# A two-block hybrid network on one core: TensorE's filler products around five of its norms are left out

## The chip, the core and the metric

The kernel runs on one core of a Trainium2 chip, in one launch. The metric is the time of one execution on the device, in microseconds (us). Single executions of this kernel before the change took 2808.08 to 2811.28 us. The engines are TensorE (PE in the profile, PEld for its weight loads), VectorE (DVE), ScalarE (ACT), GpSimd (POOL) and SyncE (SP), which issues the weight transfers.

## What is computed

Two blocks over one sequence of 512 tokens and 1024 channels, in float32:

```
first_block:   h = rmsnorm(x, norm_mix);  proj = h @ w_in
               mixed = gate0 * (mamba2(...) @ w_ssm_out) + gate1 * (dilated_attention(...) @ w_att_out)
               x = x + mixed @ w_mix_out
               h = rmsnorm(x, norm_ffn)
               x = x + (silu(h @ w_ffn_gate) * (h @ w_ffn_up)) @ w_ffn_down
               x = rmsnorm(x, norm_final)                              # norm 2
second_block:  a = diff_attention(rms_norm(h, a_norm_pre)) @ w_o
               h = h + rms_norm(a, a_norm_post)                        # norm 4
               f = conv_ffn(rms_norm(h, ffn_norm_pre[0]))
               h = h + rms_norm(f, ffn_norm_post[0])                   # norm 6
               a = forgetting_attention(rms_norm(h, b_norm_pre), k, v, c) @ w_o
               h = h + rms_norm(a, b_norm_post)                        # norm 8
               f = conv_ffn(rms_norm(h, ffn_norm_pre[1]))
               out = h + rms_norm(f, ffn_norm_post[1])                 # norm 10
rmsnorm(x, g) = x * rsqrt(mean(x * x over channels) + eps) * g
```

The kernel counts its eleven norms from 0 to 10. The even ones from 2 on are norms of a projection's output (or, norm 2, of the stream after one); each of them but the last is followed at once by an odd norm, whose output is the operand of the next projection.

## The kernel before

Activations stay in SBUF with channels on the partitions: XT is 8 chunks of 128 channels by 512 tokens. A projection runs in panels of 256 output columns; its weights come in slabs of two chunks (SyncE, into `raw`), and GpSimd splits each slab into a rounded high part `whi` (L556) and the rest `wlo` (L558), in four slots. TensorE makes each product of float32 operands as three (high by high, low by high, high by low), so a chunk of a panel is six products of 128x512 (L598, in `chunk`). A slot comes free when TensorE is through with the slab (`slab_done`), and only then does GpSimd split the next.

The order on each engine is written out by hand; semaphores join the engines. Around an even norm k it is as follows. After each panel of the projection VectorE takes the result out of PSUM (L1721 for norm 2, L1760, to `branch`, for the others), ScalarE squares it (L991) and VectorE adds the squares in `acc` (L1341). TensorE then sums acc over the partitions in `sum_squares` (L655, AUX bank 3), ScalarE takes the root (`std`, L999), VectorE the reciprocal (`rstd_col`, L1348), and TensorE spreads the factors over the partitions in `spread` (L667, AUX bank 3 again). Then comes a chain over the eight chunks. In norm 2 VectorE scales the chunk in place (XT, L1752); in the others it scales the branch (L1765) and adds it to the stream (XT, L1767). ScalarE makes the high part of the next operand (`opA_hi`, L995) and the squares for the odd norm; VectorE makes the low part (`opA_lo`, L1332) and adds the squares. That is three VectorE operations a chunk in norm 2 and four or five in norms 4, 6 and 8; in norm 10 two, and the chunk is stored.

TensorE takes the chunks as they come, in `twin_mm`, which runs two panels side by side so that each chunk of the operand feeds both (for norm 6 the second panel is the narrow one of the forget gates). After the first panel's last chunk it makes the odd norm's sum_squares, then the second panel's last two chunks, then the odd norm's spread.

`keep_warm(n)` issues n products of an identity with the attention mask (both bfloat16, 128x512) into an AUX bank that nothing reads then. They wait for nothing and nothing waits for them, but TensorE's queue is in order, so what stands behind waits until they are through. `branch_norm` puts 14 before sum_squares, 15 between sum_squares and spread and 14 after spread. Other calls put 9 behind the odd norms' spread and 7 in places of the attention stages; six products of another kind start the kernel.

Of the kernel before, what the change touches and what calls it, by code (L numbers as in the profile page):

```python
# [23 lines left out]
WARM_SQUARES, WARM_FACTORS, WARM_RESIDUAL, WARM_BANKS, WARM_UNIT = 14, 15, 14, 9, 7  # L24
# [224 lines left out]
def build(nc, I, out):  # L249
    ctx = ExitStack()  # L250
    with ctx:
# [318 lines left out]
        def _(pe):  # L570
# [78 lines left out]
            def sum_squares(k):  # L649

                if k == 0:
                    pe.wait_ge(first_in, 16 * N_FIRST)
                pe.wait_ge(acc_ready, DC * (k + 1))
                for t in range(NB):
                    last = nc.tensor.matmul(AUX[:, 3, t:t + 1], acc[:, t * P:(t + 1) * P], ones[:, 0:1], start=True, stop=True)  # L655
                last.then_inc(ss_done, 1)

            def keep_warm(n, bank=0):

                for _ in range(n):  # L660
                    nc.tensor.matmul(AUX[:, bank, :], ident_bf[:], mask1[:, 0:S], start=True, stop=True)  # L661

            def spread(k):

                pe.wait_ge(rstd_ready, k + 1)
                for t in range(NB):
                    last = nc.tensor.matmul(AUX[:, 3, t * P:(t + 1) * P], rstd_col[:, t:t + 1].broadcast_to([P, P]), ident[:], start=True, stop=True)  # L667
                last.then_inc(bc_done, 1)

            def branch_norm(k):  # L670

                keep_warm(WARM_SQUARES)
                sum_squares(k)
                keep_warm(WARM_FACTORS)
                spread(k)
                keep_warm(WARM_RESIDUAL)

            def after_norm(key, k, panels):

# [164 lines left out]
            for n in range(4):  # L844
                panel_mm("down1", n)
            branch_norm(2)


# [78 lines left out]
            for n in range(2, 4):  # L927
                panel_mm("awo", n)
            branch_norm(4)
            after_norm(("fin", 0), 5, 2 * FP)  # L930
            for n in range(4):
                panel_mm(("fout", 0), n)
            branch_norm(6)

            twin_mm(("k3", 0), 7)
# [1037 lines left out]
```

## Time and profile before

| | us |
|---|---|
| median of three runs (2808.08, 2810.1, 2811.28) | 2810.1 |
| the profiled execution's own time | 2811.09 |
| its span in the trace | 2809.3 |
| TensorE busy | 2638.3 (94%) |
| GpSimd busy | 1616.1 (58%) |
| VectorE busy | 1479.3 (53%) |
| ScalarE busy | 705.3 (25%) |
| mean granted TensorE clock, share of full | 0.964 |

The page gives each engine's busy time as a share of the span, and below that the chain of work that ended last: from the last instruction back, at each step to what released it. A share of the chain by line says how much of the span hangs on that line. Busy shares are means over stages with different limits, so what a change in one stage is worth is read in that stage, in the order of time. Times in rows are from the start of the span. The ends of TensorE's products are modelled: rows of neighbouring products overlap, and their distance from start to start is their rate. A product of float32 operands that is not split takes two or more passes, so the four products of sum_squares and of spread are eight records each. Some records of products are missing.

### The profile page before, as it was taken

Reading aid. Unit: us, or ns where it says so; the run is one execution under the profiler, and the core shown is the slowest. Engines: PE = TensorE matmul, PEld = TensorE weight load, DVE = VectorE, ACT = ScalarE, POOL = GpSimd, SP = SyncE. Lnnn points to the kernel's source line nnn. Section 1 sums busy time; section 2 is a strip of 40 time slices with the busy share of each in tenths; the row PEclk is TensorE's granted clock in tenths of the full one; section 3 lists DMA queues with packets and bytes.
Section 4 is the critical chain, followed back from the end, with each engine's and each line's share of the span. In section 5 each row is a group of like instructions: output and inputs, shape, how many; then the busy total and the mean of one; then the engine's idle time right before and its main releaser. Section 6 shows DMA issues by size and latency. Waiting matters only on the chain.

```text
span 2809.3 us, 37473 instructions
## 1 busy us (share of the span) xinstructions
PE 2638.3 (94%) x12925; PEld 2135.0 (76%) x12948; DVE 1479.3 (53%) x2085; ACT 705.3 (25%) x1251; POOL 1616.1 (58%) x1548
## 2 busy tenths in 40 slices
PE   8878889998999999999999799999989999999998
PEld 6667777787877878888777568888766776688886
DVE  5677677453423523320467668882164445687722
ACT  2233333101123111110234424331022222233300
POOL 5534454574444767777544257887653332588874
PEclk9989899999999999999999899999999999999999
DMA  4433232232222333333312123333221211233331
GB/s 136 121 79 85 70 94 80 75 95 63 68 59 65 117 89 97 96 99 95 101 61 64 35 65 89 96 97 98 76 72 61 61 61 35 63 97 97 96 97 58
DMA packets 235781, 229.17 MB, mean 82 GB/s; under 512 B 15808, under 2 KB 228288, under 8 KB 235664
## 3 DMA queue, kind: packets, MB, share of 16 engines
q1 hardware_dynamic: 212224, 204.72, 25.3%
q10 hardware_dynamic: 23440, 22.82, 2.9%
q8 instruction: 82, 1.34, 0.2%
q14 instruction: 35, 0.29, 0.0%
HBM read 222.67 MB, written 4.82 MB: 81 GB/s over the span
## 4 chain that ended last, share of the span: by engine, by line
PE 72%; DVE 7%; issue 2%; ACT 1%; DVEq 0%; ACTq 0%
PE PS L598 57%; PE PS L592 5%; PE AUX L861 2%; PE AUX L910 1%; PE AUX L813 1%; DVE acc L1341 1%; PE AUX L661 1%; PE AUX L900 1%; DVE opA_lo L1332 1%; DVE branch L1765 1%; PE AUX L915 1%; PE AUX L832 1%; PE AUX L822 0%; PE AUX L864 0%; PE AUX L655 0%
## 5 line engine op out<-in xcount | busy, mean ns | idle before, releaser
L556 POOL TENSOR_SCALAR whi<-raw 128x512 fp32r<-128x512 f32 x772 | 557.0, 722 | 1097.2 <-issue 546.6
L558 POOL TENSOR_TENSOR wlo<-raw,whi 128x512 fp32r<-128x512 f32 x772 | 1059.9, 1373 | 64.5
L598 PE MATMUL PS<-opA_hi,whi 128*128 128x512 f32 x1904 | 764.1, 401 | 34.5 <-DVE opA_lo L1332 22.0
L598 PE MATMUL PS<-opA_hi,wlo 128*128 128x512 f32 x1904 | 749.1, 393 | 0.0
L598 PE MATMUL PS<-opA_lo,whi 128*128 128x512 f32 x1904 | 748.5, 393 | 0.0
L598 PEld LDWEIGHTS PS<-opA_hi,whi 128*128 128x128 f32 x1904 | 362.6, 190 | 128.8 <-DVE opA_lo L1332 22.3
L598 PEld LDWEIGHTS PS<-opA_hi,wlo 128*128 128x128 f32 x1904 | 361.5, 190 | 77.8
L598 PEld LDWEIGHTS PS<-opA_lo,whi 128*128 128x128 f32 x1904 | 362.5, 190 | 72.6 <-issue 0.9
L1789 DVE SCALAR_TENSOR_TENSOR facc<-fu,vec,facc 128x512 f32<-128x512 f32 x176 | 202.1, 1204 | 52.7 <-ACT facc L1221 52.7
L592 PE MATMUL PS<-whi,opA_hi 128*128 128x256 f32 x704 | 211.1, 300 | 1.4 <-DVE y_ssm L1559 1.0
L598 PE MATMUL PS<-hid_hi,whi 128*128 128x512 f32 x528 | 205.4, 389 | 0.0
L598 PE MATMUL PS<-hid_lo,whi 128*128 128x512 f32 x528 | 205.4, 389 | 0.0
L598 PE MATMUL PS<-hid_hi,wlo 128*128 128x512 f32 x528 | 205.4, 389 | 0.0
L592 PE MATMUL PS<-whi,opA_lo 128*128 128x256 f32 x704 | 203.3, 289 | 0.0
L592 PE MATMUL PS<-wlo,opA_hi 128*128 128x256 f32 x704 | 203.0, 288 | 0.0
L592 PEld LDWEIGHTS PS<-whi,opA_hi 128*128 128x128 f32 x704 | 140.1, 199 | 10.3 <-issue 5.6
L592 PEld LDWEIGHTS PS<-whi,opA_lo 128*128 128x128 f32 x704 | 139.8, 199 | 2.4 <-issue 2.3
L1760 DVE COPY branch<-PS 128x512 f32<-128x512 f32 x32 | 20.6, 686 | 227.8 <-PE PS L598 227.8
L592 PEld LDWEIGHTS PS<-wlo,opA_hi 128*128 128x128 f32 x704 | 139.3, 198 | 0.0
L1249 ACT ACTIVATE sc<-sc,bstat 128x128 f32<-128x128 f32 (+3 forms) x128 | 70.8, 554 | 208.1 <-DVE bstat L1850 208.1
L598 PEld LDWEIGHTS PS<-hid_hi,wlo 128*128 128x128 f32 x528 | 99.1, 188 | 20.7
L598 PEld LDWEIGHTS PS<-hid_lo,whi 128*128 128x128 f32 x528 | 99.1, 188 | 20.5
(282 smaller groups left out, 3482.3 us busy)
## 6 DMA issues: line engine op xcount, KB each, us to landing
raw<-in_w_in_dram SPq DMA_DIRECT2D x184, 256.0 KB, 2.7
raw<-in_ffn_w_in_dram SPq DMA_DIRECT2D x176, 256.0 KB, 2.7
raw<-in_ffn_w_out_dram SPq DMA_DIRECT2D x88, 256.0 KB, 2.8
raw<-in_a_w_qkv_dram SPq DMA_DIRECT2D x48, 256.0 KB, 2.7
raw<-in_w_ffn_gate_dram SPq DMA_DIRECT2D x44, 256.0 KB, 2.8
raw<-in_w_ffn_up_dram SPq DMA_DIRECT2D x44, 256.0 KB, 2.7
raw<-in_w_ffn_down_dram SPq DMA_DIRECT2D x44, 256.0 KB, 2.7
acs_row<-acs_dram ACTq DMA_DIRECT2D x16, 512.0 KB, 5.7
```

The costliest lines, as they stand in the source:

```text
L556: nc.gpsimd.tensor_scalar(whi[slot][:], raw[raw_slot][:], 1.0, 1.0, ALU.mult, ALU.mult).then_inc(w_high, 1)
L558: nc.gpsimd.tensor_tensor(wlo[slot][:], raw[raw_slot][:], whi[slot][:].bitcast(F32), ALU.subtract).then_inc(slab_split, 1)
L592: last = nc.tensor.matmul(psum_tm(key, panel)[:, t, :], a, b[:, c, :], start=t % 2 == 0 and k + n == 0, stop=k == total - 1 and n == 2, sk ...
L598: last = nc.tensor.matmul(psum_fm(key, panel, m), a, b[:, k, :], start=k + n == 0, stop=k == total - 1 and n == 2)
L661: nc.tensor.matmul(AUX[:, bank, :], ident_bf[:], mask1[:, 0:S], start=True, stop=True)
L813: nc.tensor.matmul(AUX[:, bank, 0:width], q1[j][:, 2 * gi + hh, q0:q0 + P], k1[j][:, 2 * gi + hh, k0:k0 + width], start=True, stop=False)
L832: last = nc.tensor.matmul(AUX[:, 2, 0:P], probT[:, n, :], v1[j][:, b, gi * PANEL + hh * P:gi * PANEL + (hh + 1) * P], start=n == 0, stop=n ...
L861: last = nc.tensor.matmul(AUX[:, e, 0:width], q2[j % 2][rows, hh, q0:q0 + P], k2[j % 2][rows, hh, 0:width], start=True, stop=True)
L900: last = nc.tensor.transpose(AUX[:, 2 + e, b * P:(b + 1) * P], src, ident[:])
L910: last = nc.tensor.matmul(AUX[:, 2, e * 64:e * 64 + 64], pT[:, e, b, :], v2[j % 2][:, b, hh * P + e * 64:hh * P + e * 64 + 64], start=b == ...
L1249: A(sc[:, u % 2, e, 0:width], sc[:, u % 2, e, 0:width], ACT.Exp, bias=bstat[:, u % 4, 2 + e:3 + e], accum_out=bstat[:, u % 4, 4 + e:5 + e] ...
L1789: V.scalar_tensor_tensor(facc[:, j, :], fu[:, j, tap:tap + S], col("ffn_conv_w_2", 132 * l + 44 * tap + FT * half + m + 2 * i), facc[:, j, ...
```

## The change

The three calls of keep_warm in `branch_norm` are left out. branch_norm is called for norms 2, 4, 6, 8 and 10. The fillers of the odd norms and of the attention stages stay.

```diff
             def branch_norm(k):
 
-                keep_warm(WARM_SQUARES)
                 sum_squares(k)
-                keep_warm(WARM_FACTORS)
                 spread(k)
-                keep_warm(WARM_RESIDUAL)
```

TensorE's order at norm 2, behind down1, before the change (whi and wlo are slots of split weights, hid the hidden activations, opA the next operand):

```order
L598 MATMUL PS<-hid_hi_146,wlo3_64 128x512
L661 MATMUL AUX<-mask1_83,ident_bf_84 128x512 x14
L655 MATMUL AUX<-ones_69,acc_72 128x1 x4
L661 MATMUL AUX<-mask1_83,ident_bf_84 128x512 x15
L667 MATMUL AUX<-ident_68,rstd_col_75 128x128 x4
L661 MATMUL AUX<-mask1_83,ident_bf_84 128x512 x14
L598 MATMUL PS<-opA_hi_65,whi0_57 128x512
```

The same place in TensorE's order after it:

```order
L598 MATMUL PS<-hid_hi_146,wlo3_64 128x512
L655 MATMUL AUX<-ones_69,acc_72 128x1 x4
L667 MATMUL AUX<-ident_68,rstd_col_75 128x128 x4
L598 MATMUL PS<-opA_hi_65,whi0_57 128x512
```

Norms 4, 6 and 8 read alike, norm 10 without the last row. No other engine's order has moved, and the sums, the spread and the products of the projections stand in the order in which they stood.

## Rows read from the trace of the kernel before

**Rows 1.** The page: busy time and instructions by engine; the chain by line.
```profile
PE 2638.3 (94%) x12925; PEld 2135.0 (76%) x12948; DVE 1479.3 (53%) x2085; ACT 705.3 (25%) x1251; POOL 1616.1 (58%) x1548
...
PE PS L598 57%; PE PS L592 5%; PE AUX L861 2%; PE AUX L910 1%; PE AUX L813 1%; DVE acc L1341 1%; PE AUX L661 1%; PE AUX L900 1%; DVE opA_lo L1332 1%; DVE branch L1765 1%; PE AUX L915 1%; PE AUX L832 1%; PE AUX L822 0%; PE AUX L864 0%; PE AUX L655 0%
```
**Rows 2.** The chain in order of time at norm 2: start, us, what.
```profile
1344.91 4.77 PE PS L598 x21
...
1354.30 3.26 PE AUX L661 x15
```
**Rows 3.** TensorE's timeline at norms 2 and 3: start us, us, engine, line, operation.
```profile
1349.74 2.97 PE L661 MATMUL AUX<-mask,ident_bf 128*128 128x512 bf16 x13
1353.24 1.05 PE L655 MATMUL AUX<-ones,acc 128*128 128x1 f32 x8 [0.54 <-DVE acc L1341]
...
1357.39 1.05 PE L667 MATMUL AUX<-ident,rstd_col 128*128 128x128 f32 x8
...
1381.66 0.50 PE L598 MATMUL PS<-opA_hi,whi 128*128 128x512 f32 x1 [0.99 <-DVE opA_lo L1332]
...
1383.35 1.05 PE L655 MATMUL AUX<-ones,acc 128*128 128x1 f32 x8
```
**Rows 4.** VectorE's timeline at norms 2 and 3.
```profile
1351.09 2.10 DVE L1341 TENSOR_TENSOR acc<-acc,sq 128x512 f32<-128x512 f32 x2
1354.61 0.18 DVE L1348 RECIPROCAL rstd_col<-std 128x4 f32<-128x4 f32 x1 [1.42 <-ACT std L999]
1358.48 0.75 DVE L1752 SCALAR_TENSOR_TENSOR XT<-XT,vec,AUX 128x512 f32<-128x512 f32 x1 [3.70 <-PE AUX L667]
...
1360.09 0.75 DVE L1332 SCALAR_TENSOR_TENSOR opA_lo<-XT,vec,opA_hi 128x512 fp32r<-128x512 f32 x1
...
1375.44 1.78 DVE L1341 TENSOR_TENSOR acc<-acc,sq 128x512 f32<-128x512 f32 x1
```
**Rows 5.** TensorE's timeline at norm 10.
```profile
2789.70 1.05 PE L655 MATMUL AUX<-ones,acc 128*128 128x1 f32 x8
...
2793.84 1.05 PE L667 MATMUL AUX<-ident,rstd_col 128*128 128x128 f32 x8
```
**Rows 6.** VectorE's timeline at norm 10.
```profile
2788.15 1.49 DVE L1341 TENSOR_TENSOR acc<-acc,sq 128x512 f32<-128x512 f32 x2
2790.99 0.18 DVE L1348 RECIPROCAL rstd_col<-std 128x4 f32<-128x4 f32 x1 [1.35 <-ACT std L999]
```
**Rows 7.** TensorE's timeline at norms 4 and 5, two waits.
```profile
1658.00 0.50 PE L598 MATMUL PS<-opA_hi,whi 128*128 128x512 f32 x1 [0.70 <-DVE opA_lo L1332]
...
1666.10 0.50 PE L598 MATMUL PS<-opA_hi,whi 128*128 128x512 f32 x1 [1.99 <-DVE opA_lo L1332]
```
**Rows 8.** Stretches: length, busy us of PE, PEld, DVE, ACT, POOL; granted clock; DMA.
```profile
200.60:205.00 4.40, 0.01 (x1) 0.00 (x0) 4.40 (x6) 0.63 (x2) 2.21 (x2) 0.79 0.32 103
203.12:213.36 10.24, 7.56 (x29) 6.16 (x30) 2.87 (x6) 2.46 (x4) 0.00 (x0) 0.50 0.08 26
...
1349.70:1361.10 11.40, 10.77 (x57) 5.81 (x58) 5.90 (x9) 5.50 (x9) 1.90 (x2) 1.00 0.16 46
...
89.70:94.90 5.20, 0.04 (x1) 0.00 (x0) 5.10 (x5) 1.28 (x3) 5.03 (x5) 0.90 0.37 100
93.90:100.70 6.80, 5.76 (x16) 4.63 (x17) 4.60 (x13) 2.96 (x6) 1.43 (x1) 0.50 0.25 74
...
1402.50:1404.10 1.60, 0.00 (x0) 0.00 (x0) 1.57 (x5) 0.00 (x0) 1.52 (x2) 1.00 0.51 156
1404.61:1408.03 3.42, 3.08 (x9) 1.09 (x8) 2.33 (x7) 0.88 (x4) 0.00 (x0) 0.50 0.24 77
```
**Rows 9.** TensorE's timeline at norm 7, a stretch at the low clock.
```profile
2067.21 0.63 PE L598 MATMUL PS<-opA_hi,wlo 128*128 128x512 f32 x1
2067.64 1.70 PE L655 MATMUL AUX<-ones,acc 128*128 128x1 f32 x8
...
2071.90 1.88 PE L667 MATMUL AUX<-ident,rstd_col 128*128 128x128 f32 x8
```

## Prediction, written before the changed kernel ran

> **What bounds the kernel now.** I read the page's share of engines first: TensorE is busy for 94% of the span and the matmuls of line 598 alone make 57% of the chain that ended last [rows 1]. So the end is set by TensorE's products, and only what makes those start later, or run slower, counts. The change takes products away that feed nothing, so next I read the chain in the order of time around one of the norms, norm 2 [rows 2]. The reader is to see 3.26 us of filler (L661 x15, the second group) standing in it as a piece of its own, between sum_squares and spread. This filler is on the chain. The first group is not: there the chain runs over VectorE and ScalarE (XT, sq, acc). The third group is not either: after spread the chain goes to VectorE (XT), ScalarE (opA_hi) and VectorE (opA_lo).
>
> **What the change does, group by group.** There are five norms, 43 fillers each, 215 in all. In the order, a row of 14, a row of 15 and a row of 14 go; nothing else moves and no wait is added or removed.
>
> First group (14, before sum_squares). In norm 2 the 14 products run from 1349.74 to 1352.71, and the sums at 1353.24 still wait 0.54 us for VectorE's acc [rows 3]. Norms 4, 6 and 8 show the same wait. In the last norm the filler ends with acc: acc ends at 2788.15 + 1.49 = 2789.64 and the sums start at 2789.70, the 0.05 us hand-over that is also seen elsewhere (acc ends 1351.09 + 2.10 = 1353.19, sums 1353.24) [rows 3 to 6]. So this group is worth 0 in all five; VectorE's accumulation covers it.
>
> Second group (15, before spread). The reciprocal that spread needs ends at 1354.61 + 0.18 = 1354.79; spread starts at 1357.39. With 0.05 us of hand-over, the filler holds it up by 2.60 - 0.05 = 2.55 us [rows 3, 4]. In the last norm it is 2793.84 - (2790.99 + 0.18) - 0.05 = 2.62 us [rows 5, 6]; norms 4, 6 and 8 read as the last one does. Sum: 2.55 + 4 x 2.62 = **13.0 us**, all of it on the chain.
>
> Third group (14, after spread). Spread starts at 1357.39 [rows 3] and is over a little before VectorE's first operation at 1358.48; 14 products at the 0.216 us of the other groups (2.97 us for 13 records, one of the 14 is missing) then fill it to 1361.1. The first product (L598) could start when its opA_lo is there, at 1360.09 + 0.75 = 1360.84 [rows 4]: 0.2 us in norm 2. In norms 4, 6 and 8 the first product already waits for opA_lo behind the filler, so 0. In the last norm nothing of TensorE follows. Beyond the start, the products that follow are paced by VectorE (below), so I take 0 for all of it.
>
> **What the filler covered: TensorE's clock.** Without it TensorE is idle from the last projection product to the sums (3.5 us in norm 2: 1349.74 to 1353.24), works for 1 us, is idle for 0.6 us, works for 1 us and is idle for about 2.5 us until opA_lo. In that stretch, as in the other four, the granted clock is now 1.00, the 2.4 GHz level [rows 8]. What happens after an idle stretch, other places of this trace show: after 5.2 us without work (89.7 to 94.9) the clock is 0.50, the 1.2 GHz level, from 93.9 to 100.7, so for 5.8 us of the work that follows; after 4.4 us (200.6 to 205.0) from 203.1 to 213.4; after only 1.6 us (1402.5 to 1404.1) from 1404.6 to 1408.0 [rows 8]. So the low level comes 2.1 to 4.2 us after the idle time began and stays for 3.9 to 8.4 us of the work behind it, 6.0 in the mean of these three. I expect it in all five norms.
>
> The Trainium skill (TensorE: Matmul & The Clock Gate, section HAM oscillation — how this bites in real kernels) speaks against this change: idle time between bursts drops the clock and the next burst pays for it, half of the throttled time. By it, with all of that payment on the chain, the sum below would shrink to the last norm's share; rival (2) prices just that from rows.
>
> Its price on the chain, part by part. The sums take 1.05 us at the full clock, 1.70 at the low one; spread 1.05 and 1.88 [rows 3, 9]: +0.65 and +0.83. The sums come 3.5 us after the idle time begins, between those 2.1 and 4.2, so half of the 0.65 is taken (0.3 us); spread comes at 5.1 us, later than both, so most of the 0.83 (0.7 us). Bounds per norm: 0 and 1.48 us; taken **1.0 us**. So each norm starts its residual 2.6 - 1.0 = 1.6 us earlier.
>
> The products behind. At the full clock they follow each other by 0.227 us (4.77 us for 21 of them, [rows 2]), at the low one by 0.43 (the last before the sums at 2067.21, the sums at 2067.64, [rows 9]). 3.9 to 8.4 us at the low clock hold 9 to 20 of them, late by 0.20 each: 1.8 to 4.0 us. Do they set the pace there? In norm 4 (as in 8 and 6) no: they wait for opA_lo, 0.70 us at 1658.0 and 1.99 us at 1666.1 [rows 7], which takes up 2.7 us within the first 14 us, and more waits of the kind follow. So VectorE's chain sets the end, and it moves by the whole 1.6 us. In norm 2 VectorE has three operations a chunk instead of five and TensorE is nearly full: from the first product (1361.1) it waits three times, the longest 0.99 us, up to the sums of norm 3 at 1383.35 [rows 3]. New estimate for it: first product at 1360.84 - 1.6 + 0.05 = 1359.3; 6.0 us at the low clock give 14 of the 84 products before the sums, the other 70 take 15.9 us: 1381.2, which is 2.1 us earlier than 1383.3. VectorE can follow: it is slow (1.78 us an addition) where it works beside GpSimd [rows 4], GpSimd starts only when slabs of weights are used up, and slower products put that off, not forward. Bounds for norm 2, by 8.4 and 3.9 us at the low clock: 1.0 and 3.1; taken **2.1 us**.
>
> **Sum.** Norm 2: 2.1. Norms 4, 6, 8: 3 x 1.6 = 4.8. Norm 10: 1.6; behind it is only VectorE's chain and the store. Together 8.5 us. The profiled execution took 2811.09 us, 1.0 above the median of 2810.1; 2811.1 - 8.5 = 2802.6, and against the median 2801.6. I forecast **2801.6 us**.
>
> **Rivals.**
> (1) The clock does not fall, since the two bursts of 1 us break the idle time. Then all 13.0 + 0.2 us are gained: 2797. For it: not every wait for opA_lo in norms 4 and 8 is followed by a low stretch. Against it: the 1.6 us gap of [rows 8] was enough, and the idle share here is far larger.
> (2) The four gains are lost behind the spread: products at the low clock set the pace of the stage, or a stage's start falls earlier on GpSimd's work and VectorE is slowed for longer. Price: the 4.0 us of late products after 8.4 us at the low level are more than each 1.6; only the last norm's 1.6 us is left: 2808.5. For it: norm 2 has less than 3 us of waiting to give. Against it: the waits of 2.7 us and more in the others.
> (3) Slower. The clock is low at the end of the stage. There the last 18 products, the sums and spread are on TensorE alone, and norm 6 shows it: the sums and spread of norm 7 behind it stand at 1.70 and 1.88 us [rows 9], after VectorE had kept TensorE waiting. In norms 2, 4 and 8 it is not paid now; it would be 18 x 0.20 + 0.65 + 0.83 = 5.1 us each. It decides from two of three on (10.2 against the gain of 8.5); all three give 2810.1 - 8.5 + 15.3 = 2816.9. For it: cold starts change where the waits for VectorE fall. Against it: the last products come 18 us and more after the cold start, and no low stretch of [rows 8] outlasts the idle time by more than 8.4 us; late products close waits instead of opening them.
> (4) That the fillers still run is excluded: their rows are gone from the order.
>
> **How the numbers follow.** What cannot be told from no change is 0.2%, 5.6 us, so faster means below 2804.5. Forecast 0.60 (own range 2798 to 2806, mostly faster: 0.55), (1) 0.12, (2) 0.20, (3) 0.08. Faster 0.67, same 0.26, slower 0.07. Low end of the range: 13.0 us and 1 us more from norm 2 (its 3.1 against 2.1, and less work beside GpSimd), 2796. High end: rival (2), 2809. Elsewhere low stretches of the attention stages will fall at other places than now, since everything is shifted; the three runs of before span 3.2 us, which includes this.
>
> **What would show it.** Right: L661 with 82 to 101 records instead of 297; between the reciprocal and spread 0.05 us instead of 2.6; granted clock 0.50 over spread and the first products of each norm; L667 rows of 1.88 us; in the last norm 1.6 us less from the projection's end to the span's end; first waits for opA_lo in norms 4 and 8 smaller than 0.70 and 1.99 us. Wrong: a clock of 1.00 there (rival 1), sums of norms 3, 5, 7, 9 no earlier after the projection than now (rival 2; in norm 2 33.6 us, 1349.74 to 1383.35), or rows of 1.70 and 1.88 us at the sums and spread of norms 3, 5, 9 (rival 3).

## The result, and the profile after

The changed kernel takes 2795.73 us, the median of five runs (2790.94 to 2799.39), against 2810.43 before (2808.08 to 2811.28). The ratio is 0.9946, with a 95% interval of 0.9932 to 0.9961. That is 14.7 us less; forecast were 8.5 us less, and the time lies 0.3 us below the low end of the range. Timed again beside other kernels it was 2797.19 (2790.05 to 2798.23) against 2810.12, 12.9 us less, which lies inside the range. Two single executions, one of this kernel (7350 us) and one of a kernel below (6273 us), took more than twice as long as the others and are left out of the ranges given; the two medians would be 0.3 us lower without them. So the direction was forecast rightly and the size was not: 4 to 6 us more came than the sum had.

The page of the changed kernel, first lines and the chain by line:

```profile
span 2793.9 us, 37053 instructions
...
PE 2593.6 (93%) x12720; PEld 2117.6 (76%) x12733; DVE 1482.1 (53%) x2085; ACT 705.2 (25%) x1251; POOL 1619.3 (58%) x1548
...
PE PS L598 57%; PE PS L592 5%; PE AUX L858 2%; DVE acc L1338 1%; PE AUX L907 1%; PE AUX L810 1%; DVE opA_lo L1329 1%; PE AUX L897 1%; DVE branch L1762 1%; PE AUX L912 1%; PE AUX L829 1%; PE AUX L667 1%; DVE bstat L1845 0%; PE AUX L655 0%; PE AUX L819 0%
```

Against [rows 1] TensorE has 205 matmul records less and 45 us less busy time; the bound is the same. The filler has left the chain. Its pieces at norm 2, in the order of time (start, us, what):

```profile
1351.75 1.74 PE AUX L655 x8
1353.52 0.18 ACT std L996
...
1353.79 0.19 DVE rstd_col L1345
...
1354.02 2.09 PE AUX L667 x8
1356.14 0.76 DVE XT L1749
```

Where [rows 2] has 3.26 us of filler, the chain now goes from the sums over ScalarE's root and VectorE's reciprocal straight to spread. TensorE's timeline at norms 2, 4, 6, 8 and 10 and then at norm 7 (start, us, engine, line, operation, idle time before and what ended it):

```profile
1351.75 1.73 PE L655 MATMUL AUX<-ones,acc 128*128 128x1 f32 x8 [3.57 <-DVE acc L1338]
1354.02 2.08 PE L667 MATMUL AUX<-ident,rstd_col 128*128 128x128 f32 x8 [0.54 <-DVE rstd_col L1345]
...
1641.13 1.05 PE L655 MATMUL AUX<-ones,acc 128*128 128x1 f32 x8 [3.57 <-DVE acc L1338]
1642.66 2.07 PE L667 MATMUL AUX<-ident,rstd_col 128*128 128x128 f32 x8 [0.47 <-DVE rstd_col L1345]
...
2023.68 1.27 PE L655 MATMUL AUX<-ones,acc 128*128 128x1 f32 x8 [3.56 <-DVE acc L1338]
2025.43 2.08 PE L667 MATMUL AUX<-ident,rstd_col 128*128 128x128 f32 x8 [0.47 <-DVE rstd_col L1345]
...
2393.75 1.87 PE L655 MATMUL AUX<-ones,acc 128*128 128x1 f32 x8 [3.57 <-DVE acc L1338]
2396.09 2.08 PE L667 MATMUL AUX<-ident,rstd_col 128*128 128x128 f32 x8 [0.47 <-DVE rstd_col L1345]
...
2776.49 1.05 PE L655 MATMUL AUX<-ones,acc 128*128 128x1 f32 x8 [2.97 <-DVE acc L1338]
2778.02 1.48 PE L667 MATMUL AUX<-ident,rstd_col 128*128 128x128 f32 x8 [0.47 <-DVE rstd_col L1345]
...
2057.50 0.95 PE L655 MATMUL AUX<-ones,acc 128*128 128x1 f32 x8
2059.80 1.05 PE L667 MATMUL AUX<-ident,rstd_col 128*128 128x128 f32 x8
```

Three things are to be seen. The idle time before the sums is 3.0 to 3.6 us now, where [rows 3] has 0.54. Spread takes 2.08 us at four norms and 1.48 at the last: the clock is low there, as forecast (by how much is left to see below). And the last two lines are norm 7, where [rows 9] has 1.70 and 1.88 us: there the clock was low before and is not any more, at a norm that no edit touches. The granted clock of three of the stretches (length, busy time of PE, PEld, DVE, ACT, POOL, then clock, DMA share, GB/s):

```profile
1351.80:1362.00 10.20, 7.12 (x24) 6.09 (x25) 5.87 (x10) 5.37 (x10) 0.00 (x0) 0.51 0.07 22
1642.00:1652.20 10.20, 6.46 (x20) 5.24 (x20) 7.34 (x13) 3.86 (x7) 0.00 (x0) 0.50 0.00 1
...
2393.00:2406.50 13.50, 9.01 (x28) 7.59 (x29) 8.86 (x15) 4.38 (x8) 0.00 (x0) 0.50 0.06 19
```

They were at 1.00 [rows 8]. The low level begins 3 to 5 us after TensorE fell idle and lasts until 3.4 to 5.1 us after the first product of the next projection (1358.64 at norm 2).

Where the 15.4 us between the two spans lie is read from the starts and ends of the sums and spreads of the eleven norms in both traces. "Norm 2 to 3" is from the start of norm 2's sums to the end of norm 3's spread, and "norm 3 to 4" from there to the next sums:

| stretch, us | before | before, second trace | changed | changed, second trace | change, first traces |
|---|---|---|---|---|---|
| start to the sums of norm 1 | 1005.1 | 999.3 | 1003.7 | 1003.5 | -1.5 |
| norm 2 to 3 | 34.9 | 34.9 | 33.4 | 33.3 | -1.5 |
| norm 3 to 4 | 257.7 | 257.7 | 256.0 | 256.1 | -1.7 |
| norm 4 to 5 | 40.6 | 40.6 | 39.0 | 39.0 | -1.6 |
| norm 6 to 7 | 43.8 | 43.8 | 37.2 | 38.9 | -6.6 |
| norm 7 to 8 | 332.7 | 332.9 | 332.9 | 325.1 | +0.2 |
| norm 8 to 9 | 40.2 | 40.2 | 39.8 | 39.8 | -0.4 |
| norm 10 to the end | 19.6 | 19.6 | 17.4 | 18.0 | -2.2 |
| norms 1 to 2, 5 to 6, 9 to 10 | | | | | 0.1 at most each |

The five norms of the edit give 12.3 us, of which 6.6 at norm 6 alone; the other 3.1 us come from stretches with no edit in them. In the second traces norm 6 gives 4.9 us and norm 7 to 8 another 7.8. They are of the experiments below.

The stretches that differ are those with the low clock in them. Norms 1 to 2, 5 to 6 and 9 to 10 have a mean granted clock of 1.00 in all fourteen traces of this document and repeat within 0.1 us, but for what two edits add there. Here is norm 7 to 8 (columns as above) in both traces of the changed kernel, and then in the kernel below with 8 fillers added:

```profile
2060.85:2393.75 332.90, 311.92 (x1694) 239.26 (x1695) 147.92 (x336) 74.48 (x199) 117.64 (x121) 0.96 0.20 62
2062.48:2387.54 325.06, 305.04 (x1696) 235.93 (x1696) 147.88 (x336) 74.39 (x199) 117.71 (x121) 0.98 0.21 63
```

```profile
2066.54:2402.53 335.99, 317.97 (x1709) 243.09 (x1710) 147.90 (x336) 74.45 (x199) 117.56 (x122) 0.95 0.21 61
```

Added up from the granted clock of the traces, the low level takes 28, 15 and 34 us of these three. Over all fourteen the stretch is 325.1 us long with 15 us of it, 328.9 to 331.0 with 17 to 24, 332.7 to 332.9 with 28 to 31 and 336.0 with 34. So how long this stretch lasts goes with how much of it falls to the low clock; what decides that was not tried.

### The profile page after: what moved, and what is told of

Read it like the earlier page. It is cut to its first block, busy times and chain, and to the rows that moved or that the text cites. A ratio compares the mean times of both kernels' runs of the same rounds, so it can differ in the third digit from the quotient of the medians.

```text
span 2793.9 us, 37053 instructions
## 1 busy us (share of the span) xinstructions
PE 2593.6 (93%) x12720; PEld 2117.6 (76%) x12733; DVE 1482.1 (53%) x2085; ACT 705.2 (25%) x1251; POOL 1619.3 (58%) x1548
## 4 chain that ended last, share of the span: by engine, by line
PE 72%; DVE 8%; issue 2%; ACT 1%; DVEq 0%; ACTq 0%
PE PS L598 57%; PE PS L592 5%; PE AUX L858 2%; DVE acc L1338 1%; PE AUX L907 1%; PE AUX L810 1%; DVE opA_lo L1329 1%; PE AUX L897 1%; DVE branch L1762 1%; PE AUX L912 1%; PE AUX L829 1%; PE AUX L667 1%; DVE bstat L1845 0%; PE AUX L655 0%; PE AUX L819 0%
## 5 line engine op out<-in xcount | busy, mean ns | idle before, releaser
L598 PEld LDWEIGHTS PS<-hid_hi,whi 128*128 128x128 f32 x528 | 99.1, 188 | 20.6
## 6 DMA issues: line engine op xcount, KB each, us to landing
raw<-in_w_in_dram SPq DMA_DIRECT2D x184, 256.0 KB, 2.7
raw<-in_ffn_w_in_dram SPq DMA_DIRECT2D x176, 256.0 KB, 2.7
raw<-in_ffn_w_out_dram SPq DMA_DIRECT2D x88, 256.0 KB, 2.6
raw<-in_a_w_qkv_dram SPq DMA_DIRECT2D x48, 256.0 KB, 2.8
raw<-in_w_ffn_gate_dram SPq DMA_DIRECT2D x44, 256.0 KB, 2.7
raw<-in_w_ffn_up_dram SPq DMA_DIRECT2D x44, 256.0 KB, 2.7
raw<-in_w_ffn_down_dram SPq DMA_DIRECT2D x44, 256.0 KB, 2.6
```

Source lines behind the costliest of these rows:

```text
L598: last = nc.tensor.matmul(psum_fm(key, panel, m), a, b[:, k, :], start=k + n == 0, stop=k == total - 1 and n == 2)
```

## The experiments

Theory A is the prediction's: the 15 fillers are on the chain, the clock falls in their absence and takes a part back, the rest is chance. Against it stood B (all of the difference is a repeatable effect of the edit), C (the low clock helps) and F (the low clock behind norm 6 costs nothing), and for the excess at norms 6 and 7, D (made locally, by norm 6's fillers) against E (made by where the clock's changes stand, which anything ahead of them moves).

**The kernel before, once more.** No edit.

> The kernel before, unchanged, for a second trace of it. Theory A (the prediction's mechanism, plus chance in where the low clock falls): the distances that no edit touches move by 1 to 3 us from one execution to the next, among them the first 1005 us of the span (1005.1 in the first trace of before, 1003.6 in that of the changed kernel), and the low clock at the end of norm 7 (sums 1.70, spread 1.88 us) may be there or not. Theory B (all of the 14.7 us is the edit's doing): this trace repeats the first one within 0.3 us at every norm, the low clock at the end of norm 7 included. Time 2808 to 2812.

Measured: 2805.33 us for the profiled execution; the 17 runs of before that were timed with it spread over 2804.36 to 2811.44. The first 1005 us are 5.9 us shorter than in the first trace, as A wants. But behind norm 1 everything up to norm 7 repeats the first trace within 0.05 us, as B wants, and the slow end is there again. TensorE's timeline at norm 7 in this trace:

```profile
2061.75 1.70 PE L655 MATMUL AUX<-ones,acc 128*128 128x1 f32 x8
...
2066.02 1.86 PE L667 MATMUL AUX<-ident,rstd_col 128*128 128x128 f32 x8
```

So it was a fixture of the kernel before, not chance, though the kernel does the same work in the first stage in anything from 999.3 to 1007.6 us (over all traces below).

**The changed kernel, once more.** No further edit.

> The changed kernel again, for a second trace and five more times. Theory A: 2790 to 2800 as before, with single executions 4 to 8 us apart; in the distances between norms that no edit touches (start to norm 1, norm 3 to norm 4, norm 7 to norm 8) differences of 1 to 3 us from the first trace. Theory B: the second trace repeats the first within 0.3 us at each norm.

Measured: 2797.19 us, ratio 0.9957 (0.9944 to 0.9970). Norms 2 to 5 repeat within 0.15 us, norm 6 to 7 is 1.8 us longer and norm 7 to 8 is 7.8 us shorter than in the first trace. So the gains at norms 2 and 4 and between 3 and 4 are the edit's, and single stretches behind norm 6 move by several us from execution to execution.

**Only the 15 between the sums and the spread left out.**

```diff
                 sum_squares(k)
-                keep_warm(WARM_FACTORS)
                 spread(k)
```

> Only the 15 fillers between the sums and the spread are left out, at all five norms; the 14 before and the 14 behind stay. Theory A: TensorE's clock stays at the full level around the norms (idle time of about 0.6 us only), spread takes 1.05 us and starts 2.6 us earlier: 5 x 2.6 = 13 us less than before, 2797, and about 4 to 5 us less than the changed kernel by the norms alone (the 1.0 us of slow sums and spread per norm). Theory C (the low clock helps, since slower products start GpSimd later beside VectorE's chain): not faster than the changed kernel, 2796 to 2800, with sums of the next norm later after the spread than in the changed kernel.

Measured: 2793.98 us, ratio 0.9945 (0.9932 to 0.9958), 3.2 us less than the changed kernel timed beside it (A had 4 to 5, and 2797 for the time). TensorE's timeline at norm 2 and at norm 4:

```profile
1351.08 1.05 PE L655 MATMUL AUX<-ones,acc 128*128 128x1 f32 x8 [0.54 <-DVE acc L1340]
1352.68 1.16 PE L667 MATMUL AUX<-ident,rstd_col 128*128 128x128 f32 x8 [0.54 <-DVE rstd_col L1347]
...
1639.82 1.05 PE L655 MATMUL AUX<-ones,acc 128*128 128x1 f32 x8 [0.54 <-DVE acc L1340]
1641.34 2.07 PE L667 MATMUL AUX<-ident,rstd_col 128*128 128x128 f32 x8 [0.47 <-DVE rstd_col L1347]
```

Spread starts 1.52 to 1.60 us after the sums instead of 4.15: the 2.6 us that the sum gave to each group of 15 are confirmed at all five norms. C is wrong in the sum: with the clock mostly up the stages are as short or shorter (norm 2 to 3: 32.5 us against 33.4), and the time is below C's 2796 to 2800. But its sign is there in part: at norm 2 the next sums come 0.6 us later after the spread than in the changed kernel. VectorE's chain there, from the end of spread to the end of the last opA_lo, takes 22.8 us in the four traces in which the products come late (both of the changed kernel, and two kernels below), 23.2 in all others but the one with the 15 alone (21.7); GpSimd is busy beside it for 13.2 to 14.0 us instead of 14.6. So late products do give a little back, less than the slow sums and spread cost. At norm 4 the clock falls all the same, though TensorE is idle there for 0.54 and 0.47 us only, with nothing but sums of one column between; A had not expected that.

**Only the 15 kept.** The two outer calls of keep_warm are left out.

> Only the 15 fillers between the sums and the spread stay; the 14 before the sums and the 14 behind the spread are left out. Theory A: the 15 fillers still hold spread up, and since TensorE was idle for 3.5 us before the sums, part of them runs at the low clock, at 0.43 instead of 0.216 us each: spread starts 0 to 3.2 us later than before at each norm, so the kernel is as fast as before or slower, 2810 to 2822. Rival (the two outer groups cost time on the chain too): faster than before by over 3 us.

Measured: 2814.80 us, ratio 1.0019 (1.0010 to 1.0027): slower, as A says. TensorE's timeline at norm 2:

```profile
1353.00 1.73 PE L655 MATMUL AUX<-ones,acc 128*128 128x1 f32 x8 [3.57 <-DVE acc L1339]
1354.96 5.68 PE L661 MATMUL AUX<-mask,ident_bf 128*128 128x512 bf16 x14 [0.24 <-issue]
1360.48 1.05 PE L667 MATMUL AUX<-ident,rstd_col 128*128 128x128 f32 x8
```

The 15 last 5.7 us here where they last 3.4 at the full clock, and the sums to the spread take 7.5 us. At norm 2, where nothing was edited ahead, this is the work of the missing 14 before the sums: they cover nothing on the chain, but they decide what the following 15 cost.

**Two instead of 15**, the outer groups kept.

```diff
-                keep_warm(WARM_FACTORS)
+                keep_warm(2)
```

> At all five norms the fillers between the sums and the spread are 2 instead of 15; the 14 before and the 14 behind stay. In the trace without any of the 15, spread started 1.53 to 1.60 us after the sums, of which 0.5 us idle, and the clock still fell for one low stretch at two of the five norms. Theory A: two fillers (0.43 us) fit into the idle time, spread starts at 1.5 to 1.7 us after the sums, and the clock stays up at the spread at more of the norms: 2790 to 2795, equal to leaving the 15 out or up to 3 us faster. Rival: what is put there costs its own time, 5 x 0.43 = 2.2 us slower than leaving the 15 out, 2796.

Measured: **2787.96 us** (2786.73 to 2788.92), ratio 0.9919 (0.9906 to 0.9933), the fastest of all, and 22.8 us less than before. TensorE's timeline at norm 2:

```profile
1353.09 1.05 PE L655 MATMUL AUX<-ones,acc 128*128 128x1 f32 x8 [0.54 <-DVE acc L1341]
1354.00 0.59 PE L661 MATMUL AUX<-mask,ident_bf 128*128 128x512 bf16 x2
1354.68 1.16 PE L667 MATMUL AUX<-ident,rstd_col 128*128 128x128 f32 x8
```

The two fit between the sums and the reciprocal: spread starts 1.59 us after the sums, as with none, and takes 1.16 us at all five norms, norm 4 among them. In its trace the stretches of the five norms are shorter than before by 2.5, 2.5, 8.1, 2.1 and 2.5 us. It was 6.0 us faster than the kernel without the 15, more than the forecast 3; the two profiled executions differ by only 0.2 us in span (1.0 and 1.6 us less at norms 4 and 6, 0.4 more at norm 8 and 2.0 more in the first stage), and where the rest of the 6 us lies in the other runs was not traced. Their mean granted clocks point to the low clock: 0.967 in the four other executions without the 15 (2793.7 to 2794.6 us), 0.969 in the traced one (2789.1), and 0.968 to 0.970 in all five with two.

**The low clock behind norm 6.** Three edits: fillers left out at norm 6 alone; at the four others alone; and none left out, but 8 or 14 more behind norm 5's spread, which only moves what follows.

```diff
             def after_norm(key, k, panels):
 ...
-                    keep_warm(WARM_BANKS)
+                    keep_warm(WARM_BANKS + 8 * (k == 5))
```

> All three groups of fillers are left out at norm 6 alone. Theory D (the low clock at the end of norm 7 is made locally, by where VectorE's chain, GpSimd's splitting and TensorE's waits fall between norms 6 and 7): from the sums of norm 6 to the end of norm 7's spread 37 to 39 us instead of 43.8, everything before norm 6 as in the two traces of before (257.7 us from norm 3 to norm 4), time 2803 to 2806. Rival E (it is made by how the clock's changes stand at norm 6, which the norms before decide): 42 us or more there, time 2808.

> All three groups are left out at norms 2, 4, 8 and 10 and kept at norm 6. Theory D: from the sums of norm 6 to the end of norm 7's spread 43.8 us as before; norms 2, 4, 8 and 10 as in the changed kernel (1.5, 1.6, 0.4 and 2.0 us less than before), from norm 3 to norm 4 1.6 us less than before; time 2801 to 2804. Rival E: 37 to 42 us there, time 2797 to 2800.

> The kernel before with 8 more fillers (1.7 us at the full clock) behind the spread of norm 5 only; the distance from norm 5 to norm 6 grows by about 1 us, and nothing at norms 6 and 7 is edited. Theory E (the slow end of norm 7 in before hangs on when the clock falls and rises there, which whatever is moved ahead of it decides): from the sums of norm 6 to the end of norm 7's spread 37 to 41 us instead of 43.8, with sums to spread of norm 7 at 2.3 and spread at 1.05 us, so 2 to 4 us faster than before although work is added. Rival D (it is made by the fillers of norm 6): 43.8 us again, 1 us slower than before, 2811.

> As the one with 8 more fillers, with 14 (3.0 us) behind the spread of norm 5; the distance from norm 5 to norm 6 grows by about 2.5 us. Theory E: the slow end of norm 7 is gone or there, by where the clock's changes now stand (another place than with 8), so either about 2 us faster or 2.5 us slower than before. Rival D: 43.8 us from norm 6 to norm 7 again, 2813.

Measured:

| left out or added | time, us | ratio to before, interval | norm 6 to 7, us | sums to spread, spread of norm 7 |
|---|---|---|---|---|
| nothing | 2809.7 to 2810.7 | | 43.8 | 4.3, 1.9 |
| norm 6's fillers | 2800.54 | 0.9965 (0.9952 to 0.9979) | 38.4 | 2.4, 1.05 |
| the others' fillers | 2796.52 | 0.9948 (0.9934 to 0.9961) | 39.8 | 2.3, 1.05 |
| 8 added at norm 5 | 2807.09 | 0.9991 (0.9982 to 1.0000) | 38.2 | 2.3, 1.05 |
| 14 added at norm 5 | 2805.06 | 0.9984 (0.9974 to 0.9993) | 39.8 | 2.3, 1.05 |

TensorE's timeline at norms 6 and 7 of the kernel with 8 added, where nothing at these norms is edited:

```profile
2028.36 1.05 PE L655 MATMUL AUX<-ones,acc 128*128 128x1 f32 x8 [0.53 <-DVE acc L1341]
2029.27 3.40 PE L661 MATMUL AUX<-mask,ident_bf 128*128 128x512 bf16 x15
2032.51 1.05 PE L667 MATMUL AUX<-ident,rstd_col 128*128 128x128 f32 x8
...
2063.24 0.95 PE L655 MATMUL AUX<-ones,acc 128*128 128x1 f32 x8
2065.49 1.05 PE L667 MATMUL AUX<-ident,rstd_col 128*128 128x128 f32 x8
```

Neither theory holds as it was worded. With the fillers left out at norm 6 alone the stretch is 38.4 us, inside D's 37 to 39 and not E's 42 or more, and the time is 2.5 us below D's range. With the others' left out it is 39.8 us where D wanted 43.8, which is E's, and with norm 6 as before and only the distance to it moved it is 5.6 and 4.0 us shorter. So the slow end needs no edit at norm 6 to go away, which refutes D, and an edit at norm 6 takes it away too, which refutes E's "the norms before decide". What is left is that any of these moves took it away.

VectorE's last opA_lo cuts the stretch in three: from the sums of norm 6 to the end of its spread, from there VectorE's chain to the end of the last opA_lo, and what TensorE does alone behind it, to the end of norm 7's spread. That opA_lo before and with 8 added, in VectorE's timeline:

```profile
2063.09 1.76 DVE L1332 SCALAR_TENSOR_TENSOR opA_lo<-XT,vec,opA_hi 128x512 fp32r<-128x512 f32 x1
```

```profile
2059.85 1.10 DVE L1332 SCALAR_TENSOR_TENSOR opA_lo<-XT,vec,opA_hi 128x512 fp32r<-128x512 f32 x1
```

| norm 6 to 7, us | sums and spread | VectorE's chain | TensorE alone | together |
|---|---|---|---|---|
| before (both traces) | 5.2 | 29.7 | 8.9 | 43.8 |
| changed | 3.8 | 28.4 | 4.9 | 37.2 |
| changed, second trace | 3.8 | 29.6 | 5.5 | 38.9 |
| norm 6's fillers out | 4.4 | 28.8 | 5.2 | 38.4 |
| the others' fillers out | 5.2 | 29.7 | 4.9 | 39.8 |
| 8 added at norm 5 | 5.2 | 27.4 | 5.6 | 38.2 |
| 14 added at norm 5 | 5.2 | 29.7 | 4.9 | 39.8 |

The slow end is the third part: 3.3 to 4.0 us are gone from it each time. The chain is another matter. It comes out at 27.4 to 29.7 us, VectorE is busy in all but 0.5 us of it, and its operations take 1.1 to 1.8 us instead of 0.7 while GpSimd splits beside it (10 operations of GpSimd in the 27.4 us, 12 in the 29.7). The granted clock around norm 7's sums shows what differs in the third part; first the second trace of before, then the kernel with 8 added:

```profile
2057.70:2067.90 10.20, 9.56 (x30) 7.60 (x30) 2.05 (x3) 0.17 (x1) 4.01 (x5) 0.51 0.17 57
```

```profile
2057.40:2060.80 3.40, 3.40 (x10) 2.66 (x9) 3.37 (x5) 1.25 (x2) 1.32 (x2) 0.51 0.08 29
2063.30:2066.50 3.20, 3.20 (x23) 2.93 (x23) 0.18 (x1) 0.17 (x1) 3.12 (x4) 1.00 0.43 142
```

In before the clock falls 4 us ahead of the sums (2061.75) and stays low for 10.2 us, over sums and spread; moved by one us, it falls 5.8 us ahead (2063.24), is low for 3.4 us and up again in time. With more work in it the kernel is no slower, and with 14 added it is faster by 0.07 to 0.26%. The whole 4.0 to 5.6 us do not arrive: the added fillers make norm 5 to 6 longer by 1.0 and 2.3 us, and norm 7 to 8 takes 336.0 us with 8 added instead of 332.7 (329.9 with 14). With the others' fillers out and norm 6 as before, 4.0 of the 6.6 us are there too. What is left for norm 6's own fillers is 0.9 to 2.6 us (39.8 against 37.2 and 38.9 in the changed kernel), around the 1.6 of the forecast; its sums and spread alone give 1.4.

**Fillers where the clock falls.** The kernel before, with four fillers ahead of each wait for opA_lo from the fourth chunk on, between norms 6 and 7 only.

```diff
                     if t == a:
+                        if norm == 7 and c > 2:
+                            keep_warm(4)
                         pe.wait_ge(ready, base + c + 1)
```

> The kernel before with four fillers (0.86 us) ahead of each wait for opA_lo from the fourth chunk on, in the stage between norms 6 and 7 only. Theory A: the clock stays up there, sums and spread of norm 7 take 0.95 and 1.05 us instead of 1.70 and 1.88, sums to spread 2.3 instead of 4.3; with the products of the last chunks at the full rate 4 to 6 us less than before, 2805. Rival F (the slow end costs nothing, VectorE's chain ends as late anyway): sums to end of spread shorter by 2.8 us at most, the sums not earlier, 2807 to 2810.

Measured: 2806.53 us (2798.06 to 2810.69, twelve runs, six of them over 2807), ratio 0.9987 (0.9977 to 0.9997). The median is 3.1 us less than before, short of A's 4 to 6 and just below F's range, so the stretch has to decide: norm 6 to 7 takes 39.3 us, sums and spread of norm 7 1.05 us each, and the sums come 1.8 us earlier after those of norm 6, where F wanted them no earlier. TensorE's part alone is 5.2 us instead of 8.9 and VectorE's chain 28.9 instead of 29.7: 3.8 of the 4.5 us were the low clock's directly, which is A and not F. In the trace norm 7 to 8 took 336.0 us, so 3.3 us of it went again behind. The same four in the kernel with two fillers:

> Two fillers instead of 15 between sums and spread at the five norms (2788.0 us before this), and the four fillers ahead of the waits from the fourth chunk on between norms 6 and 7. That kernel shows no low clock at norm 7's sums and spread any more, so theory A expects no gain from the added fillers: the same within 2 us, 2786 to 2790. Rival F is not touched by this one; if it were over 2 us faster, products before the sums at the low clock would still be on the chain.

Measured: 2790.28 us, ratio 0.9930 (0.9918 to 0.9943), 2.3 us more than without them and 0.3 above the range. Norm 6 to 7 is 36.8 us against 35.7: where the clock is up at the end anyway, they only cost.

**Only the 14 behind the spread kept.**

> The fillers before the sums and between sums and spread are left out at all five norms; the 14 behind the spread stay. Sums and spread are slow as in the changed kernel (1.5 to 2.3 and 2.07 us). Theory A: at the low clock 14 fillers last 6 us, so they hold up the first product, which is free 2.5 to 3.3 us after the spread, by up to 3 us; behind it VectorE's chain sets the pace in norms 4, 6 and 8, so the time is that of the changed kernel or up to 3 us more, 2796 to 2800. Rival C (late products help, since GpSimd starts later beside VectorE's chain): up to 4 us less than the changed kernel, with the sums of the next norm earlier after the spread.

Measured: 2799.08 us, ratio 0.9955 (0.9941 to 0.9969), in A's range. TensorE's timeline at norm 2:

```profile
1353.32 1.86 PE L655 MATMUL AUX<-ones,acc 128*128 128x1 f32 x8 [3.57 <-DVE acc L1339]
1355.73 2.08 PE L667 MATMUL AUX<-ident,rstd_col 128*128 128x128 f32 x8 [0.54 <-DVE rstd_col L1346]
1358.03 3.80 PE L661 MATMUL AUX<-mask,ident_bf 128*128 128x512 bf16 x13 [0.22 <-issue]
```

From the end of spread to the next sums it takes 24.3 us, as in the changed kernel (24.3): late first products are made up for in the stage behind, which VectorE paces. Neither C's gain nor a cost of 3 us a norm is seen.

## Why the prediction was right and wrong

**First and third group, 0.** Right as far as it was tried. The sums come no earlier, and keeping both outer groups with two fillers between is better than leaving all out (2788.0 against 2797.2 us). What each of the two groups does for the clock was not told apart: the third was kept alone, the first was not.

**Second group, 13.0 us.** Right, at every norm: 1.52 to 1.60 us from sums to spread where the sums run at the full clock, against 4.15.

**The clock falls at all five norms, at 1.0 us each for sums and spread.** Right in kind; the price was a little too small. From the start of the sums to the end of spread it was 5.20 us before; now 4.35, 3.60, 3.83, 4.41 and 3.01, a gain of 0.8 to 2.2 us and 1.4 in the mean, where 1.6 was taken. At norm 8 both ran wholly at the low clock, 1.87 and 2.08 us where two fillers give 1.05 and 1.16: 1.7 us, above the bound of 1.48.

**Norm 2 to 3, 2.1 us.** Measured 1.5 and 1.6, within the bounds of 1.0 to 3.1. The term for the products was right: from the first product to the sums of norm 3 it took 21.8 us (1358.64 to 1380.44) where 21.9 were forecast, though only 3.4 us of them ran at the low clock (to 1362.0) and not 6.0; of TensorE's waits one of 0.69 us was left at 1378.92 for the three of before. The 0.6 us that lack are the price at sums and spread, which gave 0.85 us here instead of 1.6.

**Norms 4, 8 and 10, 1.6 us each.** 1.6, 0.4 and 2.2 (1.6 in the second trace of norm 10). Norm 8 lacks 0.8 us at sums and spread and 0.4 us in the stage behind: VectorE's chain came out 1.5 us longer (28.9 instead of 27.4), and TensorE's part behind it 1.1 us shorter (6.5 instead of 7.6). Of the signs named, the records of L661 came (92), and smaller waits for opA_lo only in part: behind the first product 0.26 and then 2.05 us at norm 4, where 0.70 and 1.99 stood, and at norm 8 2.17 us at once.

**Norm 6, 1.6 us: this is the step that failed.** 6.6 us were measured in the first trace and 4.9 in the second. The prediction read the low clock at norm 7 from [rows 9], used it as the price of rival (3), and then let it stand in the sum as if it could only be caught by others, never lost where it was. It was 3.3 to 4.1 us of the kernel before, and it is gone in all eleven other kernels traced, with or without work added: spread of norm 7 takes 1.05 us in each, and TensorE's part behind the last opA_lo 4.9 to 5.6 us instead of 8.9. Of the 6.6 us, 1.4 are norm 6's sums and spread (forecast: 1.6), 4.0 the slow end, and 1.3 VectorE's chain, of which the second trace shows only 0.1. Norm 8 had a little of the same, 1.1 us, where rival (3) says that nothing is paid. (The stretch is still long, 42.1 us, only in the one with the 15 alone, for their own sake.)

The second wrong step was to take norm 3 to 4 as unchanged. It is 1.4 to 2.1 us shorter with every edit at norm 2 but one (258.5 us with only the 14 behind the spread kept) and stays within 0.6 us without one. The low clock goes with it: it takes 20.5 us of the stretch in all traces with 257.7 us or more, 17 us in the one with 257.1, and 10 to 14 us in those with 255.5 to 256.2. No run tried this by itself.

The sum of what was missed at norm 6 and there, less the overestimate at norms 2 and 8, 5.0 + 1.7 - 0.6 - 1.2 + 0.6 (norm 10), is 5.5 us. The rest of the 15.4 us between the two spans lies in the first stage (1.5) and is of the kind that comes and goes. That the median fell 0.3 us outside the range and the second one inside it is chance; the missed term is not.

**Rival (1)**, the clock stays up: no; with two fillers it does, and the four norms besides norm 6 then give 2.1 to 2.5 us each, close to the 2.6 of the sum. **Rival (2)**, the gains are lost behind the spread: no at norms 2 and 4, where they arrive; at norm 8 in part, since VectorE was slowed for 1.5 us longer. Little of the low clock was paid: 10.2 to 13.7 us of it behind the sums of norms 2, 4, 6 and 8 made the stages 0.9 to 1.7 us longer than with two fillers. **Rival (3)**, the low clock at the end of a stage: the mechanism is real, at 3.3 to 4.1 us for the end where 5.1 were given, but the edit took it away at the one norm that had it in full and brought it to none.

## What to carry to other kernels

Filler work on an in-order queue is free only while something else is late: size each group by the wait that it stands in (two products for 0.5 us here, not 15), and keep the group that precedes a burst, since it decides at which clock the rest runs. Before a change that moves TensorE's idle time is priced, list the low-clock stretches of the trace that lie on the chain as costs that any shift may remove or create, and widen the range by them on both sides. A kernel whose low-clock stretches repeat from trace to trace can gain from adding work, so a gain of a few us needs an experiment that only shifts.

## What the runs showed of the hardware that was not expected

- TensorE's clock fell at norm 4 of the kernel without the 15 with only 0.54 and 0.47 us of idle time around the sums of one column each (spread 2.07 us). At its other four norms, with the same idle times, spread took 1.16 us. With two fillers of 512 columns in that place it took 1.16 us at all ten norms of the two kernels traced. That the sums of one column are what let the clock fall fits this and is not shown.
- The stretches at the low clock repeat in their distance from the kernel's own events: in two traces of before, whose starts to norm 1 differ by 5.9 us, norms 2 to 7 agree within 0.05 us, the one over norm 7's sums included. After an edit they settle elsewhere.
- The first 1005 us, the same instructions in all kernels, took 999.3 to 1007.6 us over fourteen traces, and norm 7 to 8 325 to 336 us; in the traces most of the difference between two executions of one kernel is there. Norm 7 to 8 follows its time at the low clock (15 to 34 us of it); the first stage does not in all (119.5 us of it in both traces of before, 5.9 us apart), and what else moves it stays open.
